# Two transformer blocks in one kernel: stage boundaries in two halves of the tokens, a ring of four weight slabs, and modulations by row sums on VectorE

## What is computed

```python
# first_block
mods = silu(c) @ w_ada + b_ada            # 9 vectors of 1024: sh, sc, gt three times
h = rmsnorm(x, g_pre[0]) * (1 + sc1) + sh1
x = x + 0.5 * gt1 * rmsnorm(swiglu(h, w_gu1, w_dn1), g_post[0])   # 1024 -> 2*2816 -> 1024
h = rmsnorm(x, g_pre[1]) * (1 + sc2) + sh2
x = x + gt2 * rmsnorm(token_mixer(h, ...), g_post[1])  # gated linear attention + forgetting attention
h = rmsnorm(x, g_pre[2]) * (1 + sc3) + sh3
x = x + 0.5 * gt3 * rmsnorm(swiglu(h, w_gu2, w_dn2), g_post[2])
# second_block: the same three steps with its own weights, its mixer block-sparse attention
# + retention, no rmsnorm on the outputs of the steps, and a last rmsnorm:
return rmsnorm_2(h, final_norm_w)
```

## Time and profile before

| | us |
|---|---|
| median of 3 runs (lowest, highest) | 2938.03 (2936.43, 2939.3) |
| the profiled execution, its own time | 2940.38 |
| its span | 2938.6 |
| PE busy | 2712.5 (92%), 12380 records |
| DVE busy | 1355.5 (46%) |
| ACT busy | 1085.3 (37%) |
| POOL busy | 1099.6 (37%) |
| mean granted clock of TensorE | 0.953 |

### The profile page before, as it was taken

The page is one execution under the profiler, slowest core; times in us unless marked ns, Lnnn a source line. Parts: engine busy times, 40 slices in busy tenths (PEclk is TensorE's granted clock), DMA queues, the critical chain, the costliest instruction groups (busy, mean ns, idle before and its releaser), DMA issues.

```text
span 2938.6 us, 37503 instructions
## 1 busy us (share of the span) xinstructions
PE 2712.5 (92%) x12380; PEld 2140.5 (73%) x12380; DVE 1355.5 (46%) x2236; ACT 1085.3 (37%) x1541; POOL 1099.6 (37%) x490
## 2 busy tenths in 40 slices
PE   6999996898999997999996999989888989899997
PEld 3788884787777786788885888868555657688886
DVE  4677416765444135777416664231433344522222
ACT  3222224434555533322223432232665333343421
POOL 2344443323232344444444444442111223444443
PEclk9999997999999998999997999997999999999998
DMA  5545331112222232455432553322111222222232
GB/s 212 192 174 192 112 107 47 53 62 67 93 82 83 65 99 100 143 181 190 153 105 75 182 180 120 107 96 74 37 43 50 67 64 72 72 100 99 94 106 87
DMA packets 76669, 311.31 MB, mean 106 GB/s; under 512 B 8864, under 2 KB 9632, under 8 KB 67136
## 3 DMA queue, kind: packets, MB, share of 16 engines
q1 hardware_dynamic: 60480, 220.23, 22.3%
q10 hardware_dynamic: 16128, 90.28, 8.5%
HBM read 308.35 MB, written 2.13 MB: 106 GB/s over the span
## 4 chain that ended last, share of the span: by engine, by line
PE 67%; issue 22%; DVE 5%; POOL 4%; DMA 1%; ACT 0%; ACTq 0%; POOLq 0%; DVEq 0%
PE bank L1417 21%; PE bank L1419 21%; PE bank L1418 20%; POOL w_lo L387 4%; DVE h_lo L967 1%; DVE x L1009 1%; PE bank L1626 1%; PE pair L1616 1%; PE pair L1437 1%; PE bank L1634 1%; DVE adac L918 1%; PE bank L1430 1%; DVE norm_u L1002 1%; PE pair L1445 1%; DVE ssacc L934 0%
## 5 line engine op out<-in xcount | busy, mean ns | idle before, releaser
L387 POOL TENSOR_TENSOR w_lo<-raw,w_hi 128x1024 fp32r<-128x1024 f32 x420 | 1032.8, 2460 | 1711.7 <-ACT w_hi L439 1711.7
L1417 PE MATMUL bank<-h_hi,w_hi 128*128 128x512 f32 x2272 | 941.8, 415 | 48.1 <-DVE h_lo L967 24.8
L1419 PE MATMUL bank<-h_hi,w_lo 128*128 128x512 f32 x2272 | 899.5, 396 | 0.0
L1418 PE MATMUL bank<-h_lo,w_hi 128*128 128x512 f32 x2272 | 898.1, 395 | 0.0
L439 ACT ACTIVATE w_hi<-raw 128x1024 fp32r<-128x1024 f32 x420 | 445.1, 1060 | 1202.5 <-PE bank L1419 1194.7
L1417 PEld LDWEIGHTS bank<-h_hi,w_hi 128*128 128x128 f32 x2272 | 435.0, 191 | 172.8 <-issue 44.9
L1419 PEld LDWEIGHTS bank<-h_hi,w_lo 128*128 128x128 f32 x2272 | 433.9, 191 | 96.0
L1418 PEld LDWEIGHTS bank<-h_lo,w_hi 128*128 128x128 f32 x2272 | 436.0, 192 | 84.7 <-issue 5.3
L918 DVE SCALAR_TENSOR_TENSOR adac<-adaw,silu_c,adac 128x256 f32<-128x256 f32 x448 | 321.6, 718 | 16.0
L1417 PE MATMUL bank<-act_hi,w_hi 128*128 128x512 f32 x704 | 274.3, 390 | 0.0
L1418 PE MATMUL bank<-act_lo,w_hi 128*128 128x512 f32 x704 | 274.0, 389 | 0.0
(11 more groups left out here) (328 smaller groups left out, 2758.2 us busy)
## 6 DMA issues: line engine op xcount, KB each, us to landing
raw<-slabs_dram SPq DMA_DIRECT2D x420, 512.0 KB, 3.3
adaw<-ada_dram ACTq DMA_DIRECT2D x64, 1024.0 KB, 4.8
ada<-ada_dram ACTq DMA_DIRECT2D x8, 1024.0 KB, 16.2
x<-xt_dram ACTq DMA_DIRECT2D x1, 2048.0 KB, 17.6
fneg<-fneg_scratch ACTq DMA_DIRECT2D x4, 512.0 KB, 3.7
sq<-fneg_scratch ACTq DMA_DIRECT2D x4, 512.0 KB, 3.7
w<-w_dram ACTq DMA_DIRECT2D x1, 2048.0 KB, 7.3
rdec<-rdec_dram ACTq DMA_DIRECT2D x4, 512.0 KB, 3.7
```

The lines of the kernel that those rows point to most:

```text
L387: nc.gpsimd.tensor_tensor(wl[s][:], raw[:, s], wh[s][:], ALU.subtract).then_inc(lo_done, 1)
L1417: MM(out, wh[s][:, k], a, start=first and j == 0, stop=False)
L1418: MM(out, wh[s][:, k], b, start=False, stop=False)
L1419: ins = MM(out, wl[s][:, k], a, start=False, stop=end and j == len(tiles) - 1)
```

## The change

**Ring of four.** `raw`, `w_hi` and `w_lo` are rings of four slabs, and `raw` shares its memory with `w_lo` (`low` works in place). The transfer of slab c waits for PE to be done with slab c-4, and ACT makes `high` of slab c+3 after slab c.

**Modulations.** A piece is laid out as two rows of 128x1024, and each is one scalar_tensor_tensor on DVE with its row sum into `mod` (L962 of the changed kernel). The eight chained operations, `adac` and PE's ones-matmuls are gone. At the start PE no longer makes the first modulations: DVE makes two per tile of h in a loop with the tile's h_lo, and the first four slabs take each tile of h as it comes.

**Halves.** Each stage's last output tile (the last two of a mixer) is computed for tokens 0 to 255 and then for 256 to 511, and so are the first four slabs of stages 2 to 6 (`head`): 840 matmuls of 512 columns become 1680 of 256. Sum, root, reciprocal, spread, residual and norm are made for each half. `sum_out` and `spread` of the first half stand inside the second half of the last tile. At B1 to B3 (`TWO`) the second norm's sum is taken by PE straight from x² in y (`sum_new`, 16 matmuls of one column per half), not from DVE's and POOL's additions. u and h_lo go through PSUM (`scratch`), with the gain and the shift in the same operations, so POOL has nothing but its `low`s. The first two slabs of `head` go tile by tile as h comes, the third and fourth after them.

**Rest.** In mix1 the log decay of the first head is made first (one tile of 128x512 and one scan), then its distances, then the other three heads' decays. The final norm and the output are made in halves into y, with no wait for earlier output transfers.

```diff
+RING = 4
+TWO = [False, True, True, True, False, False, False]
+PLAIN = [0, 7, 6, 7, 7, 6, 7]
+SPLIT = [KT - t if t else 0 for t in PLAIN]
...
-        raw = sb("raw", [P, 2, KT, P])
-        wh = [sb(f"w_hi{s}", [P, KT, P], F32R) for s in range(2)]
-        wl = [sb(f"w_lo{s}", [P, KT, P], F32R) for s in range(2)]
+        raw, wl = [], []
+        for s in range(RING):
+            at = cursor[0]
+            raw.append(sb(f"raw{s}", [P, KT, P]))
+            cursor[0] = at
+            wl.append(sb(f"w_lo{s}", [P, KT, P], F32R))
+        wh = [sb(f"w_hi{s}", [P, KT, P], F32R) for s in range(RING)]
...
-                    sp.wait_ge(lo_done, 2 * i + s - 1)
-                    sp.dma_start(raw[:, s], W[ds(2 * i + s, 1)].rearrange("a p k n -> p (a k) n"))\
...
+                    sp.wait_ge(slab_done, RING * i + s - (RING - 1))
+                    sp.dma_start(raw[s][:], W[ds(RING * i + s, 1)].rearrange("a p k n -> p (a k) n"))\
...
+            def step(c, n=0, i=0, ahead=True):
+                act.wait_ge(slab_done, lin(c + 1, n, i))
+                if ahead:
+                    high(c + RING - 1, n, i)
...
+            def modulation(rows, b, at):
+                V.scalar_tensor_tensor(rows, rows, 1.0, silu_c[:, b], ALU.mult, ALU.mult,
+                                       accum_out=mod[:].rearrange("p b j -> p (b j)")[:, ds(at, 1)])\
+                    .then_inc(ada0_acc if isinstance(at, int) and at < 2 * ADA0 else ada_acc, 1)
...
-                chain.link(V.tensor_scalar(adac[:, s], adaw[:, s, 0], silu_c[:, b, 0:1], None, ALU.mult))
-                for k in range(1, KT):
-                    ins = V.scalar_tensor_tensor(adac[:, s], adaw[:, s, k], silu_c[:, b, k:k + 1], adac[:, s],
-                                                 ALU.mult, ALU.add)
-                    if k < KT - 1:
-                        chain.link(ins)
-                ins.then_inc(ada_acc, 1)
...
+            def norm_h(p, half, ev, rows, behind=None):
+                b, v = PRE_MOD[p]
+                hc, done = halves(half), 16 * p + 8 * half
+                dve.wait_ge(rstd_done, ev + 1)
+                if TWO[p]:
+                    dve.wait_ge(x_done, 16 * (p - 1) + 8 * half + 8)
                 def u(n):
-                    V.tensor_tensor(nu[:, n % 3], x[:, n], RSTD[:], ALU.mult).then_inc(u_done, 1)
-                u(0)
-                u(1)
+                    V.scalar_tensor_tensor(scratch(n), x[:, n, hc], pre_a[:, n:n + 1], rows[:, HALF:T], ALU.mult, ALU.mult)\
+                        .then_inc(u_done, 1)
+                for pair in range(0, KT, 2):
+                    for n in (pair, pair + 1):
+                        if pair:
+                            dve.wait_ge(h_done, done + n - 1)
+                        u(n)
+                    if behind and not pair:
+                        behind()
+                    for n in (pair, pair + 1):
+                        dve.wait_ge(hh_done, done + n + 1)
+                        V.scalar_tensor_tensor(hl[:, n, hc], scratch(n), mod[:, b, 24 * v + n:24 * v + n + 1], hh[:, n, hc],
+                                               ALU.add, ALU.subtract).then_inc(h_done, 1)
...
+                def scaled(n):
+                    V.tensor_tensor(scratch(n), y[:, n, hc], rows[:, HALF:T], ALU.mult).then_inc(y_done, 1)
+                for pair in range(0, KT, 2):
+                    for n in (pair, pair + 1):
+                        if pair:
+                            dve.wait_ge(x_done, done + n - 1)
+                        scaled(n)
+                    for n in (pair, pair + 1):
+                        dve.wait_ge(y_done, done + n + 1)
+                        V.tensor_tensor(x[:, n, hc], x[:, n, hc], scratch(n), ALU.add).then_inc(x_done, 1)
...
+            def sum_out(b, half):
+                t0 = HALF * half
+                pe.wait_ge(ssadd, SSADD[b] + PLAIN[b] - 1)
+                pe.wait_ge(sqh_done, HALVES[b] + SPLIT[b] * (half + 1))
+                src = [ssacc] + [sq[:, (PLAIN[b] + z) % 2] for z in range(SPLIT[b])]
+                for t in range(2):
+                    for j, a in enumerate(src):
+                        ins = MM(ST[:, 2 * half + t:2 * half + t + 1], a[:, t0 + P * t:t0 + P * (t + 1)], ones[:, 0:1],
+                                 start=t == 0 and j == 0, stop=j == len(src) - 1, skip_group_check=True)
+                ins.then_inc(s_sum, 1)
+            def sum_new(b, half):
+                t0 = HALF * half
+                for n in range(KT):
+                    pe.wait_ge(sx_done, 8 + 16 * (b - 1) + 8 * half + n + 1)
+                    for t in range(2):
+                        ins = MM((ST, SC1)[half][:, 4 + 2 * half + t:5 + 2 * half + t], y[:, n, t0 + P * t:t0 + P * (t + 1)], ones[:, 0:1],
+                                 start=t == 0 and n == 0, stop=n == KT - 1, skip_group_check=True)
+                ins.then_inc(s_sum, 1)
...
-                MM(b[:, 0:1], adac[:, s, 0:P], ones[:, 0:1], start=True, stop=True)
-                MM(b[:, 1:2], adac[:, s, P:2 * P], ones[:, 0:1], start=True, stop=True).then_inc(ada_cols, 1)
...
+                ev = EVENTS[b]
+                for half in range(2):
+                    hc, done, q = halves(half), 0, m + PLAIN[b] + half
+                    bank_free(q)
+                    for t in range(PLAIN[b], KT):
+                        for s in range(per):
+                            cc = c + per * t + s
+                            if half == 0:
+                                pe.wait_ge(lo_done, cc + 1)
+                            for k in parts(s):
+                                ins = triple(acc[q % 2][:, halves(t - PLAIN[b])], cc % RING, k, xh[:, KT * s + k, hc],
+                                             xl[:, KT * s + k, hc], s == 0 and k == 0, s == per - 1 and k == parts(s)[-1])
+                                done += 1
+                                if half and k == parts(s)[-1]:
+                                    ins.then_inc(slab_done, 1)
+                                if half and done == 2:
+                                    sum_out(b, 0)
+                                if half and done == 5:
+                                    spread(ev, 0, SC1)
+                    if half == 0:
+                        ins.then_inc(half_done, 1)
+                if TWO[b]:
+                    sum_new(b, 0)
+                    spread(ev + 1, 4, SC1)
+                    sum_out(b, 1)
+                elif b == LAST:
+                    sum_out(b, 1)
+                    spread(ev + 1, 2, ST)
+            def head(p, c, m, after=None):
+                banks = [bank(m), bank(m + 1), acc[m % 2], acc[(m + 1) % 2]]
...
+                for half in range(2):
+                    hc = halves(half)
+                    for k in range(KT):
+                        pe.wait_ge(h_done, 16 * p + 8 * half + k + 1)
+                        for s in range(2):
+                            if k == 0 and half == 0:
+                                pe.wait_ge(lo_done, c + s + 1)
+                            ins = triple(banks[s][:, hc], (c + s) % RING, k, hh[:, k, hc], hl[:, k, hc], k == 0, k == KT - 1)
+                            if k == KT - 1 and half:
+                                ins.then_inc(slab_done, 1)
+                        if half == 0 and k == 2:
+                            if TWO[p]:
+                                spread(ev + 2, 2, ST)
+                            else:
+                                sum_out(p, 1)
+                        if half == 0 and k == 5 and not TWO[p]:
+                            spread(ev + 1, 2, ST)
+                    for s in range(2, RING):
+                        if half == 0:
+                            pe.wait_ge(lo_done, c + s + 1)
+                            if (m + s) // 2 - 1:
+                                pe.wait_ge(acc_free[(m + s) % 2], (m + s) // 2 - 1)
+                        for k in range(KT):
+                            ins = triple(banks[s][:, hc], (c + s) % RING, k, hh[:, k, hc], hl[:, k, hc], k == 0, k == KT - 1)
+                        if half:
+                            ins.then_inc(slab_done, 1)
+                            if s == 2 and after:
+                                after()
+                    if half == 0 and TWO[p]:
+                        sum_new(p, 1)
+                        spread(ev + 3, 6, SC1)
```

More of the change, by code:

```diff
@@ L529, in ffn @@
-                if f == 1:
-                    for piece in range(2):
-                        ada_load(ADA_RUNS[2][0][2] + piece)
-                k = group_of("ffn", f)
-                out_tiles(c + 2 * FT, m + 2 * FT, 3, f < 2, k)
-                residual(f < 2, k)
-            def step(c, n=0, i=0):
-                act.wait_ge(slab_done, lin(c + 1, n, i))
-                high(c + 2, n, i)
+                    if not n:
+                        high(c + 4)
+                    for e in loads:
+                        ada_load(e, n // 2, i)
```

(23 more changed lines are left out.)

966 lines of the change are left out of this document (502 added, 464 removed), and 8 rows, old and new, of the table ADA_RUNS.

## The result

The changed kernel takes 2871.93 us (median of 4 runs, 2866.76 to 2875.45), the kernel before 2938.66 beside it (4 runs, 2936.43 to 2939.9). The ratio is 0.9772, with a 95% interval of 0.9755 to 0.979. 2836 was forecast, in a range of 2792 to 2884: the sign and the range hold, but of the 102 us that I summed up 67 came. The profiled execution's span is 2872.3 us, 66.3 under that of before; the terms are measured against that.

What follows compares the result with a forecast made beforehand. PE, busy 92% of the span, was taken to bound the kernel, so gains come from its columns or gaps. Terms of 29, 11, 18, 12, 11, 7 and 14 sum to 102: 2940.4 − 102 − 2.4 = 2836 us, range 2792 to 2884.

Steps and rivals of the forecast that it cites:

- A: FFN loops: taking modulation columns off PE saves 0.50 us a piece for 58 pieces, 29 us.
- B: Start: DVE makes modulations and h in 5.1 us steps; seventh slab at 95 instead of 106, 11 us.
- C: Boundaries 2 and 3: working in halves cuts each from about 36 us to 27, 18 us in all.
- D: Boundary 1 with mix1's head: ffn0's last matmul to first score matmul falls from 92 to 80 us, 12 us.
- E: Boundaries 4 and 5: first half's work now lies beside the second half tile; 7 and 4, 11 us.
- F: End: final operations in halves leave some 10 us behind the last matmul; gain 7 us.
- G: Ring of four: transfer, copy and `low` start two slabs earlier; 14 of 18 us of w_lo waits come back.
- The port between DVE and POOL: Rival at the start: modulations and `low` block each other, only B suffers, 8 us, 2844; counted inside the likeliest case.
- The half matmul: Price of each of 1680 matmuls of 256 columns: 118 ns, 7.6 us extra in all; bounds 113.5 to 227.
- The rival that weight loads show: Half matmuls: a 101 ns load ahead of 113 ns of columns makes 214 ns, 161 us more, 2997; chance 0.03.

Runs made afterwards that it cites:

- e3: Changed kernel with two one-column fp32 matmuls put back on PE after every second slab in the loops of three FFNs, 60 pairs; 2904.34 us.
- e1: Changed kernel with the shared region of moving operands moved 32 bytes, to begin at a multiple of 64 bytes as before; 2860.86 us.
- e2: Kernel before with the shared region of moving operands moved 32 bytes, off the multiple of 64; 2954.33 us, ratio 1.0058.
- e9: Changed kernel with the moving operands' region at a multiple of 64 bytes and the second half's squares earlier at boundary 5; 2853.86 us.
- e8: Changed kernel with the second half's last two outputs added and squared at boundary 5 before the first half's last two h tiles; 2872.84 us.
- e5: Changed kernel with ACT's decay chain at mix1's head moved ahead of the fifth slab's copy and the first value tile; 2875.93 us.
- e6: Changed kernel with the region at a multiple of 64 bytes, ACT's reordered list at mix1's head and earlier squares at boundary 5; 2858.27 us.

## Why the prediction was right, and why too large

| term | forecast | measured | how |
|---|---|---|---|
| A, modulation columns | 29 | 29 | 1.0 us ahead per 96 matmuls in the loops; e3 |
| B, the start | 11 | 4.4 | ahead at the seventh slab |
| C, boundaries 2 and 3 | 18 | 22 | 10.5 between the counts 3600 and 3900, 13.9 between 5200 and 5400, less A's part in the two, 2.5 |
| D, boundary 1 and mix1's head | 12 | 12 | 92.4 to 80.8 us, last matmul of ffn0 to first score |
| E, boundaries 4 and 5 | 11 | 6 | 7 and -1 |
| F, the end | 7 | 7 | 20.2 to 10.5 us, 2.7 lost in the half tile |
| G, the ring | 14 | 4.5 | lead over mix2 behind its head (60.3 to 63.8), and over mix1 behind its first score matmul (20.6 to 21.6) |
| not forecast: the half tile of ffn0 | 0 | -2 | lead from 11.2 to 8.9 over it |
| not forecast: place of the operand | 0 | -16 | 0.6 us per 100 matmuls of 512 columns that read the region; e1, e2 |

These make 67, the 66 of the spans within their rounding. The 35 us that are missing from 102 are 16 of the operand's place, 9.5 of G, 6.6 of B, 5 of E and 2 of the half tile, less 4 that C brought more.

*The missing term.* My sum priced every full matmul that stays as unchanged. The text read the diff for what PE computes and in what order, not for where its operands lie, though the line in `sb` is part of it. That step cost 16 of the 35 us.

*G was mis-sized, but the waits went as it said.* "A transfer, a copy and 2.4 us of `low` now start two slabs earlier" is wrong in the size: by the waits of the two kernels the copy of slab c now follows slab c-3 and not slab c-2, and in ffn3's loop it starts 10.6 us ahead of PE's slab where it started 5.1 ahead (medians of 32 slabs). One slab was enough: PE waits for w_lo in no loop and in no mixer behind its head, where ten such waits, 22.1 us in all, stood before. The 16.4 us in 9 waits that are left (rows above) lie elsewhere, 8.4 of them at the start and the others in the heads of later stages or right behind them. What failed is the step from waits to time: it took a wait that goes for time that comes back, and left the clock out. In windows of the same matmuls of mix2, the counts 7100 to 7500 and 7500 to 7900, before:

```profile
2061.90:2279.20 217.30, 186.08 (x972) 123.91 (x971) 81.59 (x381) 130.82 (x270) 39.05 (x17) 0.95 0.14 44
2279.20:2445.90 166.70, 145.18 (x610) 96.53 (x609) 65.11 (x88) 53.71 (x67) 39.25 (x17) 0.94 0.19 60
```

with the change, and last the first of them in e9:

```profile
1999.10:2222.30 223.20, 194.07 (x973) 130.12 (x972) 81.64 (x381) 130.96 (x270) 39.22 (x17) 0.91 0.14 45
2222.30:2381.90 159.60, 143.03 (x609) 95.95 (x608) 65.05 (x88) 53.70 (x67) 39.16 (x17) 0.94 0.20 64
1991.00:2207.60 216.60, 187.13 (x973) 124.27 (x972) 81.66 (x381) 130.80 (x270) 39.28 (x17) 0.95 0.14 47
```

In the later window four waits of 2.5 us for w_lo are gone, and 7.1 of their 10.1 us came back. In the earlier one the change is 5.9 us slower, though PE waits 2 us less in it: its granted clock is 0.91 for 0.95. e9 has the same ring, and the clock and the time of before. So some 6 of the 9.5 us were lost to the clock and not to the ring; why it fell there in one profile and not in the other stays open.

*B was mis-sized.* The steps took 5.2 us for my 5.1, and h was complete at 80.0 for my 78. The fifth slab then waited 5.9 us for my 3 (the row at 88.98): all four slots come free at the end of h together, and its transfer, beside three others and a modulation piece of 1 MB, took 3.8 us. The port between DVE and POOL, the rival for this term, stretched only two of the 16 row sums there (1.65 and 3.37 us for 1.21). The fifth slab's matmuls ran at the half level of the clock until 92.8 us. The seventh slab started at 101.8 for my 95.

*D was right in sum, and that is luck.* I had 9 us from the boundary and 3 from the head's shorter chain; it was 5 and 6. PE itself gained 22 us over the boundary and the head's four slabs (a lead of 8.9 at ffn0's end, 31.3 at the count 1680). But the first score matmul waits for the chain from the gate inputs, which begins when the first slab of mix1 is done for both halves, and by the order of `head` that is behind the first halves of all four slabs. ACT takes the gate inputs, before and with the change, at

```profile
485.04 0.57 ACT L554 ACTIVATE nar<-bank 48x512 f32<-48x512 f32 x1
```

```profile
470.92 0.59 ACT L604 ACTIVATE nar<-bank 48x512 f32<-48x512 f32 x1 [2.77 <-PE bank L1559]
```

That is 42.8 and 37.6 us behind ffn0's last matmul, 5 us earlier, and from there to the first score matmul it is 49.6 and 43.2 us, 6 less. Behind the head PE then stood 15.5 us in two waits (5.2 for a copy of ACT's, 10.3 for the distances, above), where it had stood 10.0 in three.

*C was right,* slightly low: per boundary 25 us for my 27. The clock is 0.80 to 0.84 across it.

*E.* Boundary 4 gave its 7. At boundary 5, I named the wait for the second half's sum "in the third tile of the head", but not that two lists keep eight tiles of h ahead of it; it ate the gain. With e8's 5.4 us the -1 of boundary 5 would be the 4 that I gave it.

*The half matmul* costs 118 to 120 ns with the clock up, for my 118. The rival that weight loads show is false at 256 columns as well. Where the Trainium skill, "TensorE: Matmul & The Clock Gate", section "The mechanism", lets a load overlap only matmuls of another row group (it also names a background weight buffer), all these read the whole array, and 101 ns of load plus 113 of columns would be 214. The trace has 118 to 120, so here the loads overlap.

## What to carry to other kernels

A buffer that shares memory with a later one is as deep as its last reader, not as its count: ask when the transfer may start, and which in-order list stands there when it hasn't ended. A sum or a root moved on one engine moves everything behind its consumer on the next, so look at that list before giving the waiting engine other work. A wait that is removed gives back less than its length (7.1 of 10.1 us here), and PE's lead at a boundary reaches a chain that starts from one slab only as far as that slab is done earlier (5 of 22 us). And print the byte offset of every moving operand of TensorE before and after an edit of the memory map or of the helper that rounds sizes: 32 bytes cost 14 us of span (e1), a fifth of this change's gain of 66.

## What the runs showed of the hardware

- A matmul of 512 fp32r columns whose moving operand begins 32 bytes past a multiple of 64 takes 233 ns from start to start, and 227 at the multiple (72 for 74 triples in 50 us, on both kernels). Only these two places were tried; at 256 columns there was no difference (118 to 120 ns).
- Two fp32 matmuls of one column between slabs cost 0.5 us (e3: 60 pairs, 29 us in the loops). From the first of their four records to the next slab's matmul it is 0.37 us, and that matmul is followed after 0.32 us in place of 0.23.
- A row sum over 128x1024 on DVE takes 1.21 us with both operands in SBUF, and up to 3.4 beside a `low` (six of 144 over 3.3).
- The granted clock differs between near relatives and between runs of one kernel. Its half level lasted 194 to 227 us in seven profiles (the changed kernel twice, e1, e5, e6, e8, e9), and 20 us more of it in one stretch of mix2 cost 6 us (223.2 for 217.3). The nine runs of the changed kernel go from 2866.76 us at a mean granted clock of 0.967 to 2882.88 at 0.959, a spread that covers the 7 us between its two medians. Why it falls in one and not in the other is left open.
